# Row-tile order at the seam between the experts and the second block, with the first q projection split by row tiles

## Chip, cores and metric

One core of a Trainium2 chip runs the whole program in one launch. The metric is device time in microseconds. The median of three runs of the kernel before is 2227.41 us.

## What is computed

Three transformer blocks on 256 tokens of width 1024, all in float32. The change lies where the first block ends and the second begins:

```python
# end of the first block (x1: the tokens ahead of the experts, y: their weighted outputs)
x = layer_norm(ALPHA * x1 + g2 * y) * post2_g + post2_b
# start of the second block
xn = rms_norm(x, norm_in_g)
proj = xn @ w_in_2                 # q, k, v, g_ret, x_lru, g_lru: 1024 columns each
q, k = rotary(q), rotary(k) * 128 ** -0.5
xc = causal_depthwise_conv(x_lru, conv_w, conv_b)          # width 4
o_lru = rg_lru(xc, gates)          # the gates are small matmuls on xc
```

## The kernel before, in words

**Tiles.** Rows are tokens. The 256 tokens are two row tiles of 128 partitions (`t` = 0, 1). A weight matrix goes through TensorE in units of 512 columns; `plan()` lists the units in the order in which SyncE loads them (2 MB each, a ring of six slots `W`) and TensorE uses them. Unit number u writes PSUM banks 0 and 1 or 2 and 3 by its parity, and starts once unit u-2 has been read (`unit_free`). `dense(name, lhs)` does one unit; `half_rows_of(name, t, lhs)` does one row tile of a unit, 8 matmuls of 128x512. A float32 matmul stands in the trace as two records, so a unit is 32 records in either form.

**The seam.** The experts leave their sum in PSUM banks 4 to 7 (bank 4+q holds columns 256q to 256q+255 of both row tiles). After the last scatter (L1087):

- VectorE takes the statistics of both tiles (L2162, L2165, L2167), ScalarE the root (`act_std`, L363), VectorE subtracts the mean and applies the gain for both tiles (L2172), then the scale and shift for both (L2178) into `X`.
- `act_rms` (L374, L376) on ScalarE squares and sums each tile of `X` and takes the root; `rms_scale` (L355, L357) on VectorE writes the normed rows to `row(2)`, and each tile raises `rows_ready`.
- TensorE transposes a tile's rows (`row_to_columns`, L797: 8 transposes into banks 4 and 5), and ScalarE copies them out as columns (`copy_columns`, L389: two copies for a tile). The first unit, `xl0`, starts at L654 when the columns of both tiles are there.
- Up to then TensorE fills its time with matmuls whose result nobody reads (`keep_active`, L803).

**Behind the seam** the units run in the order xl0, xl1, gl0, gl1, q20, q21, then eight small gate matmul pairs (L1127) that need the convolution (L2216, L2218 on VectorE, from the copied xl units), then k20 to gr1. VectorE turns q20 by its angles (`rotary`, L2234 to L2242) after the convolution. GpSimd issues the loads of the gate weights when the first block is done (`block1_done`), and of the angle table (`ROT`, L608) when both tiles have raised `rows_ready`.

The engines' programs are written out by hand and run in program order; only semaphores tie them together. `row_in` counts a tile of `X` up for ScalarE, `row_done` a tile of normed rows for TensorE:

```python
for t in range(TT):
    pe.wait_ge(ev("rows_ready"), NORMED["xn"] + t + 1)
    row_to_columns("xn", t, row(2)[:, t])
columns_ready("xn")
for n_ in ("xl0", "xl1", "gl0", "gl1", "q20", "q21"):
    dense(n_, lhs)
```

Of the kernel before, what the change touches and what calls it, by code (L numbers as in the profile page):

```python
# [17 lines left out]
ALU = mybir.AluOpType  # L18
# [3 lines left out]
T = 256  # L22
TT = T // P
D = 1024
KT = D // P
# [5 lines left out]
CONV1, CONV2 = 31, 4  # L31
# [5 lines left out]
LN_EPS, RMS_EPS = 1e-5, 1e-6  # L37
# [60 lines left out]
def plan():  # L98

    units = []  # L100

    def add(name, kind, mat, cols, rows=1):
        units.append((name, kind, [(mat, r * D, c) for c in cols for r in range(rows)]))

    def mod(name, i):
        add(name, "mod", "w_mod", [i * D, i * D + CH])

    mod("sc1", 1)
    mod("sh1", 0)
    for i in range(2):  # L110
        add(f"ag{i}", "col", "w_in", [D + i * CH])
        add(f"av{i}", "col", "w_in", [i * CH])
    for n, base in (("v", 3), ("u", 2), ("ga", 4), ("gb", 5)):
        for i in range(2):
            add(f"{n}{i}", "row", "w_in", [base * D + i * CH])
    for i in range(2):
        add(f"wb{i}", "row", "w_b", [i * CH])
    mod("g1", 2)
    for i in range(2):
        add(f"wa{i}", "row", "w_a", [i * CH])  # L120
    for i in range(2):
        add(f"wo{i}", "row", "w_out", [i * CH])
    mod("sc2", 4)
    mod("sh2", 3)
    mod("g2", 5)
    units.append(("moe", "moe", []))
    for n, base in (("xl", 4), ("gl", 5)):
        for i in range(2):
            add(f"{n}{i}", "col", "w_in_2", [base * D + i * CH])
    for n, base in (("q2", 0), ("k2", 1), ("v2", 2), ("gr", 3)):  # L130
        for i in range(2):
            add(f"{n}{i}", "row", "w_in_2", [base * D + i * CH])
    for i in range(2):
        add(f"w2o{i}", "row", "w_out_2", [i * CH], rows=2)
    add("gq", "col", "gla_w_in_3", [0])
    add("gk", "col", "gla_w_in_3", [CH])
    for i in range(4):
        add(f"gv{i}", "row", "gla_w_in_3", [D + i * CH])
    for i in range(4):
        add(f"gz{i}", "row", "gla_w_in_3", [3 * D + i * CH])  # L140
    for i in range(2):
        add(f"go{i}", "row", "gla_w_out_3", [i * CH], rows=2)
    for i in range(4):
        add(f"su{i}", "col", "s5_w_in_3", [i * CH])
    for i in range(4):
        add(f"sz{i}", "col", "s5_w_in_3", [2 * D + i * CH])
    for i in range(4):
        add(f"sg{i}", "col", "s5_w_glu_3", [i * CH], rows=2)
    for i in range(2):
        add(f"so{i}", "row", "s5_w_out_3", [i * CH], rows=2)  # L150
    return units
# [18 lines left out]
def build(nc, A, out):  # L170
# [11 lines left out]
    TB, n = {}, 0  # L182
# [8 lines left out]
    with ExitStack() as ctx:  # L191
# [33 lines left out]
        def row(i):  # L225
            return flat(i).rearrange("p (t d) -> p t d", t=TT)
# [9 lines left out]
        def pcol(r, n=1):  # L236
            return PC[:, r // P, r % P:r % P + n]
# [12 lines left out]
        def ev(name):  # L250
            if name not in S:
                S[name] = sem(name)
            return S[name]
# [44 lines left out]
        def vector(dve, name):  # L298

            n = vec_at[0]  # L300
            assert VECTORS[n][0] == name, (VECTORS[n], name)
            vec_at[0] += 1
            dve.wait_ge(v_landed[n % NV], 16 * (n // NV + 1))
            return V[:, n % NV, 0:VECTORS[n][2]]
# [34 lines left out]
        def root_taken(dve):  # L339
            norms_out[0] += 1  # L340
            dve.wait_ge(std_ready, norms_out[0])
            dve.reciprocal(RS[:], SD[:])
            dve.drain()

        def row_in(ins):

            rows_in[0] += 1
            ins.then_inc(ev("row_ready"), 1)

        def rms_scale(dve, dst, src, gain, done):  # L350

            for t in range(TT):
                norms_out[0] += 1
                dve.wait_ge(std_ready, norms_out[0])
                dve.reciprocal(RS[:, t:t + 1], SD[:, t:t + 1])  # L355
                dve.drain()
                done(dve.scalar_tensor_tensor(dst[:, t, :], src[:, t, :], RS[:, t:t + 1], gain, ALU.mult, ALU.mult))  # L357
            dve.drain()

        def act_std(act):  # L360
            norms_in[1] += 1
            act.wait_ge(var_ready, norms_in[1])
            act.activation(SD[:], VE[:], ACT.Sqrt).then_inc(std_ready, 1)  # L363

        def act_tile_std(act, t):
            norms_in[1] += 1
            act.wait_ge(var_ready, norms_in[1])
            act.activation(SD[:, t:t + 1], VE[:, t:t + 1], ACT.Sqrt).then_inc(std_ready, 1)
# [9 lines left out]
        def act_rms(act, src, unused):  # L378

            for t in range(TT):  # L380
                act_tile_rms(act, src, unused, t)
# [258 lines left out]
        def _(pe):  # L640
# [150 lines left out]
            def row_to_columns(name, t, src):  # L791
                for h in range(2):
                    n = TB[name] + 2 * t + h
                    if n >= 2:
                        pe.wait_ge(tp_copied, n - 1)
                    for j in range(4):
                        ins = pe.transpose(PS[:, 4 + n % 2, j * P:(j + 1) * P], src[:, (4 * h + j) * P:(4 * h + j + 1) * P], ident)  # L797
                    ins.then_inc(tp_ready, 1)
# [312 lines left out]
            keep_active(0, 6)  # L1111
            pe.wait_ge(ev("row_ready"), 1)
            keep_active(0, 4)
            for t in range(TT):
                pe.wait_ge(ev("rows_ready"), NORMED["xn"] + t + 1)
                row_to_columns("xn", t, row(2)[:, t])
            columns_ready("xn")
            for n_ in ("xl0", "xl1", "gl0", "gl1", "q20", "q21"):
                dense(n_, lhs)
            pe.wait_ge(ev("gate_w_landed"), 64)  # L1120
            pe.wait_ge(ev("xc_ready"), 1)
# [260 lines left out]
        def _(act):  # L1382
# [127 lines left out]
            with act.Fori(0, NE - 1) as e:  # L1510
                expert(e)
            expert(NE - 1)
            act_std(act)

            act_rms(act, X, row(3))
            copy_columns(act, "xn", col(HT))

            def quarter(name):
# [252 lines left out]
        def _(dve):  # L1771
# [6 lines left out]
            def used(ins):  # L1778
                ins.then_inc(v_used, 1)
# [377 lines left out]
            with dve.Fori(0, NE - 1) as e:  # L2157
                expert(e, False)
            expert(NE - 1, True)
            for t in range(TT):  # L2160
                for q in range(4):
                    dve.bn_stats(HST[:, 4 * t + q, :], PS[:, 4 + q, t * T:(t + 1) * T])  # L2162
            dve.drain()
            for t in range(TT):
                dve.bn_aggr(MV[:, t, :], HST[:, 4 * t:4 * t + 4, :].rearrange("p q s -> p (q s)"))  # L2165
            dve.drain()
            dve.tensor_scalar_add(VE[:], MV[:, :, 1], LN_EPS).then_inc(var_ready, 1)  # L2167
            norms_in[0] += 1
            root_taken(dve)
            vec = vector(dve, "post2_g").rearrange("p (q n) -> p q n", q=4)  # L2170
            for t in range(TT):
                ins = dve.scalar_tensor_tensor(X[:, t, :].rearrange("p (q n) -> p q n", q=4), PS[:, 4:8, t * T:(t + 1) * T],  # L2172
                                               MV[:, t, 0:1], vec, ALU.subtract, ALU.mult)
            used(ins)
            dve.drain()
            vec = vector(dve, "post2_b")
            for t in range(TT):
                row_in(dve.scalar_tensor_tensor(X[:, t, :], X[:, t, :], RS[:, t:t + 1], vec, ALU.mult, ALU.add))  # L2178
            dve.drain()
            dve.sem_inc(v_used, 1)  # L2180
            dve.sem_inc(ev("block1_done"), 1)

            def row_done(ins):
                ins.then_inc(ev("rows_ready"), 1)

            dve.wait_ge(ev("gain_landed"), 16)
            rms_scale(dve, row(2), X, TAB2[:], row_done)

            dve.wait_ge(ev("lam_ln"), 1)
            dve.tensor_scalar(LS[:, 2], LS[:, 0], 1.0, -1.0, ALU.add, ALU.add)  # L2190
# [16 lines left out]
            dve.tensor_scalar(LS[:, 4], LS[:, 1], -8.0, None, ALU.mult)  # L2207
            dve.tensor_scalar(LS[:, 5], LS[:, 1], -16.0, None, ALU.mult).then_inc(ev("rates_ready"), 1)

            dve.wait_ge(unit_free[UNIT["xl0"][0] % 2], UNIT["xl0"][0] // 2 + 1)  # L2210
            dve.wait_ge(unit_free[UNIT["xl1"][0] % 2], UNIT["xl1"][0] // 2 + 1)
            for lag in range(CONV2):
                for k in range(KT):
                    w_ = pcol(R_CW2 + (CONV2 - 1 - lag) * KT + k)
                    if lag == 0:
                        ins = dve.tensor_scalar(XC[:, k, :], XLC[:, k, :], w_, pcol(R_CB2 + k), ALU.mult, ALU.add)  # L2216
                    else:
                        ins = dve.scalar_tensor_tensor(XC[:, k, lag:], XLC[:, k, 0:T - lag], w_, XC[:, k, lag:],  # L2218
                                                       ALU.mult, ALU.add)
                if lag == CONV2 - 1:  # L2220
                    ins.then_inc(ev("xc_ready"), 1)
                dve.drain()
            dve.wait_ge(ev("tables_landed"), 80)

            def rotary(name, dst, i):
# [17 lines left out]
                    dve.drain()  # L2243

            rotary("q20", Q2, 0)
            rotary("q21", Q2, 1)
            dve.sem_inc(ev("q_ready"), 1)
            dve.wait_ge(ev("gates_read"), 8)
# [374 lines left out]
```

## Time and profile before

| | |
|---|---|
| runs | 2225.69, 2227.41, 2227.54 us (median 2227.41) |
| profiled execution | 2228.49 us, its span 2226.7 us |
| granted TensorE clock, mean | 0.991 |
| busy: PE, weight loads, DVE, ACT, POOL | 95%, 50%, 35%, 20%, 3% of the span |
| chain that ended last, by engine | PE 75%, ACT 9%, DMA 6%, DVE 5% |
| last scatter ends, first unit of block 2 starts | 1356.2 us, 1370.5 us |

PE is TensorE, DVE VectorE, ACT ScalarE, POOL GpSimd, SP SyncE. Busy time of PE includes the matmuls that nobody reads, so its 95% is not useful work. A granted clock of 1.00 is 2.4 GHz and 0.50 is 1.2 GHz.

### The profile page before, as it was taken

To read this page: it belongs to the slowest core of one execution; us is meant where nothing else is said; L and a number is where in the kernel's file an instruction comes from. 1 tells how busy PE (TensorE), PEld (TensorE's weight loads), DVE (VectorE), ACT (ScalarE), POOL (GpSimd) and SP (SyncE) were. 2 spreads that over 40 slices of the span, in tenths; PEclk is the share of its full clock that TensorE was granted. 3 is DMA by queue.
4 is the path that set the end of the run, shared out by engine and by line. 5 is a ranking of instruction groups with operands and counts; after the bars stand their busy time and mean duration, and the time that the engine had idled before them with its cause. 6 is when DMAs were issued, how large, how long until landed. Compare 5 with 4: busy or idle time off the path is not lost.

```text
span 2226.7 us, 30826 instructions
## 1 busy us (share of the span) xinstructions
PE 2122.8 (95%) x11636; PEld 1102.8 (50%) x11637; DVE 784.1 (35%) x1910; ACT 444.5 (20%) x895; POOL 76.1 (3%) x96
## 2 busy tenths in 40 slices
PE   6999999999999998999999998999999999998998
PEld 5745553333333333333333336745564446887873
DVE  1894362222222222222222223340212354998100
ACT  1011120111011110101101101132012215997100
POOL 0000000000000000000000000000000000222000
PEclk9999998999999999999999999999999999999999
DMA  9754678989999996999989999435234323232340
GB/s 368 262 189 148 247 288 324 418 342 417 372 402 419 418 418 250 417 390 374 417 354 417 418 418 379 159 114 189 76 128 151 113 95 141 78 115 77 138 156 28
DMA packets 157318, 591.33 MB, mean 266 GB/s; under 512 B 5072, under 2 KB 5136, under 8 KB 124352
## 3 DMA queue, kind: packets, MB, share of 16 engines
q1 hardware_dynamic: 152240, 572.03, 65.7%
q0 software_dynamic: 4384, 16.40, 2.0%
q10 hardware_dynamic: 624, 1.93, 0.2%
q8 instruction: 48, 0.79, 0.1%
q14 instruction: 22, 0.18, 0.0%
HBM read 589.29 MB, written 1.05 MB: 265 GB/s over the span
## 4 chain that ended last, share of the span: by engine, by line
PE 75%; ACT 9%; DMA 6%; DVE 5%; DVEq 1%; issue 1%; SPq 1%; ACTq 1%
PE PS L666 19%; PE PS L1054 15%; PE PS L654 9%; PE PS L1075 9%; DMA W<-in_w_gu 5%; PE PS L697 4%; PE PS L681 4%; PE PS L1087 2%; PE PS L1000 2%; ACT BIG L1691 1%; PE PS L1336 1%; PE PS L1045 1%; PE PS L1017 1%; DVE BIG L2076 1%; DVE BIG L2078 1%
## 5 line engine op out<-in xcount | busy, mean ns | idle before, releaser
L1054 PE MATMUL PS<-W,BIG 128*64 128x512 f32 x2048 | 451.0, 597 | 10.7 <-DMA W<-in_w_gu 10.7
L666 PE MATMUL PS<-W,BIG 128*128 128x512 f32 x960 | 417.9, 597 | 4.3 <-DVE BIG L2554 2.9
L666 PEld LDWEIGHTS PS<-W,BIG 128*128 128x128 f32 x960 | 183.2, 191 | 231.3 <-issue 225.8
L1054 PEld LDWEIGHTS PS<-W,BIG 128*64 128x64 f32 x2048 | 143.8, 137 | 300.6 <-issue 279.6
L1075 PE MATMUL PS<-W,BIG 128*64 128x512 f32 x1024 | 226.8, 595 | 2.8
L654 PE MATMUL PS<-BIG,W 128*128 128x256 f32 x896 | 194.5, 380 | 0.7 <-ACT BIG L389 0.7
L654 PEld LDWEIGHTS PS<-BIG,W 128*128 128x128 f32 x896 | 170.2, 190 | 24.5 <-ACT BIG L389 1.0
L1501 ACT ACTIVATE BIG<-BIG 128x512 f32<-128x512 f32 x32 | 20.2, 630 | 717.3 <-DVE BIG L2076 717.3
L2076 DVE TENSOR_SCALAR BIG<-PS 128x512 f32<-128x512 f32 (+1 forms) x38 | 24.7, 650 | 353.5 <-PE PS L1054 331.5
L1075 PEld LDWEIGHTS PS<-W,BIG 128*64 128x64 f32 x1024 | 70.4, 137 | 138.3 <-issue 125.0
L1273 PE MATMUL PS<-BIG,W 128*128 128x256 f32 x512 | 117.0, 382 | 5.0 <-ACT BIG L1658 3.0
L1273 PEld LDWEIGHTS PS<-BIG,W 128*128 128x128 f32 x512 | 94.9, 190 | 20.4 <-issue 7.7
L1841 DVE SCALAR_TENSOR_TENSOR BIG<-BIG,PC 128x255 f32<-128x255 f32 (+29 forms) x240 | 95.4, 464 | 3.8 <-issue 0.5
L697 PE MATMUL PS<-W,BIG 128*128 128x512 f32 x192 | 83.7, 593 | 0.7 <-ACT BIG L389 0.7
L681 PE MATMUL PS<-W,BIG 128*128 128x512 f32 x192 | 83.2, 592 | 0.0
L2118 DVE TENSOR_TENSOR BIG<-PS,BIG 128x512 f32<-128x512 f32 x32 | 22.1, 692 | 163.3 <-PE PS L1075 163.3
L958 PE MATMUL PS<-BIG 128*64 128x512 f32 x264 | 64.4, 609 | 3.9 <-issue 3.5
L1087 PE MATMUL PS<-BIG 64*128 64x256 f32 x512 | 63.9, 389 | 0.0
L1087 PEld LDWEIGHTS PS<-BIG 64*128 64x128 f32 x512 | 46.9, 186 | 30.2 <-issue 26.0
L681 PEld LDWEIGHTS PS<-W,BIG 128*128 128x128 f32 x192 | 36.4, 190 | 44.9 <-issue 44.9
L697 PEld LDWEIGHTS PS<-W,BIG 128*128 128x128 f32 x192 | 36.1, 190 | 43.5 <-issue 42.5
L2301 DVE TENSOR_TENSOR X<-X,PS 128x512 f32<-128x512 f32 x12 | 8.0, 686 | 126.0 <-PE PS L681 65.3
(508 smaller groups left out, 2012.4 us busy)
## 6 DMA issues: line engine op xcount, KB each, us to landing
W<-in_w_gu SPq DMA_DIRECT2D x128, 2048.0 KB, 15.6
W<-in_w_dn SPq DMA_DIRECT2D x64, 2048.0 KB, 16.1
W<-in_w_in SPq DMA_DIRECT2D x24, 2048.0 KB, 17.7
W<-in_w_mod SPq DMA_DIRECT2D x12, 2048.0 KB, 10.9
W<-in_gla_w_in SPq DMA_DIRECT2D x10, 2048.0 KB, 7.9
W<-in_s_w_in SPq DMA_DIRECT2D x8, 2048.0 KB, 8.8
W<-in_s_w_glu SPq DMA_DIRECT2D x8, 2048.0 KB, 8.5
W<-in_w_out SPq DMA_DIRECT2D x6, 2048.0 KB, 7.9
```

What stands on the lines that cost most here:

```text
L654: ins = pe.matmul(ps[:, m // 2, (m % 2) * T:(m % 2 + 1) * T], slot(c0 + i)[:, k, m * P:(m + 1) * P], lhs(i * KT + k), start=i + k == 0, st ...
L666: ins = pe.matmul(ps[:, t, :], lhs(i * KT + k)[:, t * P:(t + 1) * P], w[:, k, :], start=i + k == 0, stop=last_chunk and k == KT - 1)
L681: ins = pe.matmul(ps[:, t, :], lhs(i * KT + k)[:, t * P:(t + 1) * P], w[:, k, :], start=i + k == 0, stop=i == 1 and k == KT - 1)
L697: ins = pe.matmul(unit_ps(name)[:, t, :], lhs(k)[:, t * P:(t + 1) * P], slot(c0)[:, k, :], start=k == 0, stop=k == KT - 1)
L958: ins = pe.matmul(PS[hh[h], 3, :], G[:, t, :], H2[:, t, h * CH:(h + 1) * CH], start=t == 0, stop=t == TT - 1, skip_group_check=True)
L1000: ins = pe.matmul(PS[qq[q], g, 0:T], XETX[:, k, :], gu_w(k)[:, g * D + q * T:g * D + (q + 1) * T], start=False, stop=k == KT - 1, skip_gro ...
L1054: ins = pe.matmul(PS[hh[h], g, :], XET[:, k, :], gu_w(k)[:, g * D + h * CH:g * D + (h + 1) * CH], start=False, stop=k == KT - 1, skip_grou ...
L1075: ins = pe.matmul(PS[hh[h], 2, :], ACTT[:, k, :], dn_w(k)[:, h * CH:(h + 1) * CH], start=k == 0, stop=k == KT - 1, skip_group_check=True)
L1087: ins = pe.matmul(PS[:, 4 + q, t * T:(t + 1) * T], SC[r, t * P:(t + 1) * P], YE[r, (q % 2) * T:(q % 2 + 1) * T], start=False, stop=False, ...
L1273: ins = pe.matmul(PS[:, bank, part * T:(part + 1) * T], slot(c0)[:, k, m * P:(m + 1) * P], lhs(k), start=k == 0, stop=k == KT - 1, skip_gr ...
L1841: ins = dve.scalar_tensor_tensor(cv[:, k, lag:], ya[:, k, 0:T - lag], pcol(r), cv[:, k, lag:], ALU.mult, ALU.add)
L2076: dve.tensor_scalar(GT[:, w], PS[:, 0, w], 7.0, None, ALU.min).then_inc(clipped, 1)
```

## The change

- `plan()`: q20 becomes the first unit of the second block, ahead of xl0. All later units of that group but q21 move back by one place, in load order and in PSUM parity.
- VectorE does the layer norm and the RMS norm row tile by row tile: `moments(t)`, `centred(t)`, `scaled(t)`, `normed(t)` in the order m0, c0, s0, m1, c1, n0, s1, n1. ScalarE's roots follow, one for each tile.
- TensorE: transposes of tile 0, the first half of q20 (tile 0), transposes of tile 1, the second half of q20, then xl0, xl1, gl0, gl1, q21.
- VectorE: the rotation of q20 stands ahead of the convolution.

```diff
@@ plan @@
     units.append(("moe", "moe", []))
+    add("q20", "row", "w_in_2", [0])
     for n, base in (("xl", 4), ("gl", 5)):
...
     for n, base in (("q2", 0), ("k2", 1), ("v2", 2), ("gr", 3)):
-        for i in range(2):
+        for i in range(n == "q2", 2):
@@ TensorE @@
             keep_active(0, 4)
-            for t in range(TT):
-                pe.wait_ge(ev("rows_ready"), NORMED["xn"] + t + 1)
-                row_to_columns("xn", t, row(2)[:, t])
+            pe.wait_ge(ev("rows_ready"), NORMED["xn"] + 1)
+            row_to_columns("xn", 0, row(2)[:, 0])
+            pe.wait_ge(tp_copied, TB["xn"] + 2)
+            half_rows_of("q20", 0, lhs)
+            pe.wait_ge(ev("rows_ready"), NORMED["xn"] + 2)
+            row_to_columns("xn", 1, row(2)[:, 1])
             columns_ready("xn")
-            for n_ in ("xl0", "xl1", "gl0", "gl1", "q20", "q21"):
+            half_rows_of("q20", 1, lhs)
+            for n_ in ("xl0", "xl1", "gl0", "gl1", "q21"):
                 dense(n_, lhs)
@@ ScalarE @@
-            act_std(act)
-            act_rms(act, X, row(3))
+            act_tile_std(act, 0)
+            act_tile_rms(act, X, row(3), 0)
+            act_tile_std(act, 1)
+            act_tile_rms(act, X, row(3), 1)
             copy_columns(act, "xn", col(HT))
@@ VectorE @@
+            def moments(t):
+
                 for q in range(4):
                     dve.bn_stats(HST[:, 4 * t + q, :], PS[:, 4 + q, t * T:(t + 1) * T])
...
+            def centred(t):
+
+                dve.scalar_tensor_tensor(X[:, t, :].rearrange("p (q n) -> p q n", q=4), PS[:, 4:8, t * T:(t + 1) * T],
+                                         MV[:, t, 0:1], gain.rearrange("p (q n) -> p q n", q=4), ALU.subtract, ALU.mult)
...
+            moments(0)
+            centred(0)
+            scaled(0)
+            moments(1)
+            centred(1)
+            dve.wait_ge(ev("gain_landed"), 16)
...
+            normed(0)
+            scaled(1)
+            dve.drain()
+            dve.sem_inc(v_used, 2)
+            dve.sem_inc(ev("block1_done"), 1)
+            normed(1)
...
             rotary("q20", Q2, 0)
+            dve.wait_ge(unit_free[UNIT["xl0"][0] % 2], UNIT["xl0"][0] // 2 + 1)
+            dve.wait_ge(unit_free[UNIT["xl1"][0] % 2], UNIT["xl1"][0] // 2 + 1)
+            for lag in range(CONV2):
...
             rotary("q21", Q2, 1)
```

How the instructions stand now. First TensorE (PE) at the start of the second block, before: L803 is `keep_active`, L797 the transposes, L654 the matmuls of xl0. A row counts matmuls, not trace records.

```order
L803 MATMUL PS<-K 128x256 x3
L797 MATMUL PS<-K,BIG 128x128 [waits tp_copied,rows_ready]
L797 MATMUL PS<-K,BIG 128x128 x3
L797 MATMUL PS<-K,BIG 128x128 [waits tp_copied]
L797 MATMUL PS<-K,BIG 128x128 x3
L797 MATMUL PS<-K,BIG 128x128 [waits tp_copied,rows_ready]
L797 MATMUL PS<-K,BIG 128x128 x3
L797 MATMUL PS<-K,BIG 128x128 [waits tp_copied]
L797 MATMUL PS<-K,BIG 128x128 x3
L654 MATMUL PS<-BIG,W 128x256 [waits w_landed0,unit_free0,tp_copied]
```

The same place in the changed kernel, where the lines are one further down and L698 is half a unit of q20:

```order
L804 MATMUL PS<-K 128x256 x3
L798 MATMUL PS<-K,BIG 128x128 [waits tp_copied,rows_ready]
L798 MATMUL PS<-K,BIG 128x128 x3
L798 MATMUL PS<-K,BIG 128x128 [waits tp_copied]
L798 MATMUL PS<-K,BIG 128x128 x3
L698 MATMUL PS<-W,BIG 128x512 [waits w_landed0,unit_free0,tp_copied]
L698 MATMUL PS<-W,BIG 128x512 x7
L798 MATMUL PS<-K,BIG 128x128 [waits tp_copied,rows_ready]
L798 MATMUL PS<-K,BIG 128x128 x3
L798 MATMUL PS<-K,BIG 128x128 [waits tp_copied]
L798 MATMUL PS<-K,BIG 128x128 x3
L698 MATMUL PS<-W,BIG 128x512 [waits tp_copied]
```

The transposes of tile 1 have moved behind the first half of q20, and the second half waits for their copies.

ScalarE (ACT) at the same place in the changed kernel: L369 is the root of the layer norm, L375 and L377 the square sum and the root of the RMS norm, L390 the four copies of columns, L1529 the copies of xl0 and xl1.

```order
L369 ACTIVATE SD<-VE 128x1 [waits var_ready]
L375 ACTIVATE BIG,VE<-X 128x1024 [waits row_ready]
L377 ACTIVATE SD<-VE 128x1
L369 ACTIVATE SD<-VE 128x1 [waits var_ready]
L375 ACTIVATE BIG,VE<-X 128x1024 [waits row_ready]
L377 ACTIVATE SD<-VE 128x1
L390 ACTIVATE BIG<-PS 128x4x128 [waits tp_ready] x4
L1529 ACTIVATE BIG<-PS 128x1024 [waits chunk_done] x2
```

The four copies stand behind both tiles' square sums, as they did before.

VectorE (DVE) from the last scatter on in the changed kernel: L2169 to L2173 are the moments, L2180 `centred`, L2187 and L2189 `scaled`, L2205 and L2207 `normed`.

```order
L2169 BN_STATS HST<-PS 128x6 x3
L2171 BN_AGGR MV<-HST 128x2
L2173 TENSOR_SCALAR VE<-MV 128x1
L2180 SCALAR_TENSOR_TENSOR X<-PS,MV,V 128x1024
L2187 RECIPROCAL RS<-SD 128x1 [waits std_ready]
L2189 SCALAR_TENSOR_TENSOR X<-X,RS,V 128x1024
L2169 BN_STATS HST<-PS 128x6 x4
L2171 BN_AGGR MV<-HST 128x2
L2173 TENSOR_SCALAR VE<-MV 128x1
L2180 SCALAR_TENSOR_TENSOR X<-PS,MV,V 128x1024
L2205 RECIPROCAL RS<-SD 128x1 [waits std_ready,gain_landed]
L2207 SCALAR_TENSOR_TENSOR BIG<-X,RS,TAB2 128x1024
```

Tile 0's normed rows now come ahead of the scaling of tile 1, which with tile 1's own normed rows follows behind this piece.

## Rows read from the trace of the kernel before

**Rows 1.** The page: span, and the chain that ended last, by engine.

```profile
span 2226.7 us, 30826 instructions
...
PE 75%; ACT 9%; DMA 6%; DVE 5%; DVEq 1%; issue 1%; SPq 1%; ACTq 1%
```

**Rows 2.** Timeline from 1352 us: start us, us, engine line op names shapes count [idle before].

```profile
1356.25 2.75 DVE L2162 BATCH_NORM_STATS2 HST<-PS 128x6 f32<-128x256 f32 x8 [2.62 <-PE PS L1087]
1359.08 0.39 DVE L2165 BATCH_NORM_AGGREGATE MV<-HST 128x2 f32<-128x24 f32 x2
1359.55 0.17 DVE L2167 TENSOR_SCALAR VE<-MV 128x2 f32<-128x2 f32 x1
...
1360.23 2.48 DVE L2172 SCALAR_TENSOR_TENSOR X<-PS,MV,V 128x1024 f32<-128x1024 f32 x2
1362.80 2.48 DVE L2178 SCALAR_TENSOR_TENSOR X<-X,RS,V 128x1024 f32<-128x1024 f32 x2
1364.12 1.06 ACT L374 ACTIVATE BIG<-X 128x1024 f32<-128x1024 f32 x1 [4.17 <-DVE X L2178]
1364.14 2.00 PE L803 MATMUL PS<-K 128*128 128x256 f32 x8 [1.28 <-DVE X L2178]
...
1365.34 0.20 ACT L376 ACTIVATE SD<-VE 128x1 f32<-128x1 f32 x1
...
1365.64 0.16 DVE L355 RECIPROCAL RS<-SD 128x1 f32<-128x1 f32 x1 [0.36 <-ACT SD L376]
...
1365.88 1.28 DVE L357 SCALAR_TENSOR_TENSOR BIG<-X,RS,TAB 128x1024 f32<-128x1024 f32 x1
...
1367.22 1.09 PE L797 MATMUL PS<-K,BIG 128*128 128x128 f32 x8 [1.08 <-DVE BIG L357]
1367.91 1.08 ACT L389 ACTIVATE BIG<-PS 128x512 f32<-128x512 f32 x2 [1.06 <-PE PS L797]
1368.93 0.70 POOL L608 DMA_DIRECT2D TAB<-in_k_rot  x1
1369.34 1.08 ACT L389 ACTIVATE BIG<-PS 128x512 f32<-128x512 f32 x2 [0.35 <-PE PS L797]
```

**Rows 3.** The chain of waits, 1350 to 1480 us: start us, us, what.

```profile
1370.48 55.52 PE PS L654 x256
1426.00 27.47 PE PS L666 x64
```

**Rows 4.** DMA issues, 1360 to 1400 us: names, queue, count, KB, us to landing.

```profile
TAB<-in_k_rot POOLq DMA_DIRECT2D x1, 128.0 KB, 8.9
```

**Rows 5.** Timeline of VectorE behind the seam.

```profile
1402.30 9.88 DVE L2218 SCALAR_TENSOR_TENSOR BIG<-BIG,PC 128x255 f32<-128x255 f32 x24
1439.85 0.42 DVE L2234 TENSOR_TENSOR BIG<-PS,TAB 128x256 f32<-128x256 f32 x1 [27.67 <-PE PS L666]
```

**Rows 6.** Timeline of TensorE, 1795 to 1812 us.

```profile
1800.18 1.04 PE L1225 MATMUL PS<-K,BIG 128*128 128x128 f32 x8
1802.79 1.09 PE L1225 MATMUL PS<-K,BIG 128*128 128x128 f32 x8 [1.57 <-DVE BIG L2387]
1804.62 7.97 PE L666 MATMUL PS<-W,BIG 128*128 128x512 f32 x14 [0.74 <-ACT BIG L1606]
```

**Rows 7.** Stretches of 1 us: length, busy by engine, then PEclk, DMA share, GB/s.

```profile
1805.00:1806.00 1.00, 1.00 (x2) 0.34 (x1) 0.00 (x0) 0.99 (x2) 1.00 (x3) 0.51 0.00 0
...
1808.00:1809.00 1.00, 1.00 (x4) 0.37 (x3) 1.00 (x1) 0.00 (x0) 1.00 (x3) 0.79 0.93 369
```

**Rows 8.** The chain of waits, 1800 to 1836 us.

```profile
1804.62 29.43 PE PS L666 x64
```

**Rows 9.** An earlier pause of TensorE: timeline, and two stretches of 1 us.

```profile
362.67 3.68 PE L958 MATMUL PS<-BIG 128*64 128x512 f32 x8 [3.55 <-issue]
...
361.00:362.00 1.00, 0.00 (x0) 0.00 (x0) 0.00 (x0) 0.00 (x0) 0.00 (x0) 0.59 0.97 410
...
367.00:368.00 1.00, 1.00 (x6) 0.80 (x4) 0.00 (x0) 0.56 (x1) 0.00 (x0) 0.50 0.28 49
```

More of the change, by code:

```diff
@@ L2159, in _ @@
             expert(NE - 1, True)
-            for t in range(TT):
+            def moments(t):
                 for q in range(4):
                     dve.bn_stats(HST[:, 4 * t + q, :], PS[:, 4 + q, t * T:(t + 1) * T])
-            dve.drain()
-            for t in range(TT):
+                dve.drain()
                 dve.bn_aggr(MV[:, t, :], HST[:, 4 * t:4 * t + 4, :].rearrange("p q s -> p (q s)"))
-            dve.drain()
-            dve.tensor_scalar_add(VE[:], MV[:, :, 1], LN_EPS).then_inc(var_ready, 1)
@@ L2168, in _ @@
[L2168 to L2178, printed above, removed]
@@ L2179, in _ @@
-            dve.drain()
-            dve.sem_inc(v_used, 1)
-            dve.sem_inc(ev("block1_done"), 1)
+                dve.drain()
+                dve.tensor_scalar_add(VE[:, t:t + 1], MV[:, t, 1:2], LN_EPS).then_inc(var_ready, 1)
+                norms_in[0] += 1
+            gain, shift = vector(dve, "post2_g"), vector(dve, "post2_b")
+            def centred(t):
+                dve.scalar_tensor_tensor(X[:, t, :].rearrange("p (q n) -> p q n", q=4), PS[:, 4:8, t * T:(t + 1) * T],
+                                         MV[:, t, 0:1], gain.rearrange("p (q n) -> p q n", q=4), ALU.subtract, ALU.mult)
@@ L2183, in row_done, with scaled @@
+            def scaled(t):
+                norms_out[0] += 1
+                dve.wait_ge(std_ready, norms_out[0])
+                dve.reciprocal(RS[:, t:t + 1], SD[:, t:t + 1])
+                dve.drain()
+                row_in(dve.scalar_tensor_tensor(X[:, t, :], X[:, t, :], RS[:, t:t + 1], shift, ALU.mult, ALU.add))
+            moments(0)
[4 more added lines that the diff above has]
+            dve.wait_ge(ev("gain_landed"), 16)
             def row_done(ins):
@@ L2184, in row_done, with normed @@
                 ins.then_inc(ev("rows_ready"), 1)
-            dve.wait_ge(ev("gain_landed"), 16)
-            rms_scale(dve, row(2), X, TAB2[:], row_done)
+            def normed(t):
+                norms_out[0] += 1
+                dve.wait_ge(std_ready, norms_out[0])
+                dve.reciprocal(RS[:, t:t + 1], SD[:, t:t + 1])
+                dve.drain()
+                row_done(dve.scalar_tensor_tensor(row(2)[:, t, :], X[:, t, :], RS[:, t:t + 1], TAB2[:], ALU.mult, ALU.mult))
+                dve.drain()
@@ L2189, in _ @@
+            normed(0)
+            scaled(1)
+            dve.drain()
+            dve.sem_inc(v_used, 2)
+            dve.sem_inc(ev("block1_done"), 1)
+            normed(1)
             dve.wait_ge(ev("lam_ln"), 1)
@@ L2208, in _ @@
             dve.tensor_scalar(LS[:, 5], LS[:, 1], -16.0, None, ALU.mult).then_inc(ev("rates_ready"), 1)
[L2210 to L2222, printed above, removed]
             dve.wait_ge(ev("tables_landed"), 80)
@@ L2245, in _ @@
             rotary("q20", Q2, 0)
+            dve.wait_ge(unit_free[UNIT["xl0"][0] % 2], UNIT["xl0"][0] // 2 + 1)
+            dve.wait_ge(unit_free[UNIT["xl1"][0] % 2], UNIT["xl1"][0] // 2 + 1)
+            for lag in range(CONV2):
+                for k in range(KT):
+                    w_ = pcol(R_CW2 + (CONV2 - 1 - lag) * KT + k)
+                    if lag == 0:
+                        ins = dve.tensor_scalar(XC[:, k, :], XLC[:, k, :], w_, pcol(R_CB2 + k), ALU.mult, ALU.add)
+                    else:
+                        ins = dve.scalar_tensor_tensor(XC[:, k, lag:], XLC[:, k, 0:T - lag], w_, XC[:, k, lag:],
+                                                       ALU.mult, ALU.add)
+                if lag == CONV2 - 1:
+                    ins.then_inc(ev("xc_ready"), 1)
+                dve.drain()
             rotary("q21", Q2, 1)
```

## Prediction

> **What bounds the kernel now.** I read the page first: of a span of 2226.7 us the chain that ended last is 75% TensorE's, with short pieces of ScalarE and VectorE between [rows 1]. So the question is where TensorE waits and whether the edit shortens that wait. Then the timeline at the seam: the last scatter releases VectorE at 1356.25, and useful matmuls begin again at 1370.48 [rows 2, 3]. Between them lies one serial thread, 14.2 us long: statistics, two passes over X, square sum, normed rows, transposes, copies. The matmuls of L803 in it are filler. From 1370.48 on the chain is matmuls without a gap (55.52 us, then 27.47 us) [rows 3], so whatever the seam costs or saves arrives whole at the end. All other stages keep their code; their loads and waits hang on finished units and shift with them.
>
> **VectorE, tile by tile.** Eight statistics take 2.75 us, so four take about 1.4; the aggregate is about 0.26 (half of 0.39 and a start-up), the sum with epsilon 0.17, each with some 0.08 us of drain ahead [rows 2]. Moments of tile 0 end at 1356.25 + 2.0 = 1358.3. The root now runs beside `centred(0)`, which is 1.2 us (half of 2.48), to 1359.5. A reciprocal takes 0.24 to the start of its pass (1365.64 to 1365.88) and the pass 1.28: X of tile 0 is done at 1360.9. Moments of tile 1 add 1.9 (1362.8), `centred(1)` 1.2 (1364.0), `normed(0)` 1.5: tile 0's rows stand at 1365.5, against 1367.2 before. `scaled(1)` ends at 1367.0.
>
> **ScalarE, where the head start is lost.** TensorE transposes tile 0 from 1365.5, with both banks ready by 1366.6 (1.09 us [rows 2]). But in ScalarE's program the copies stand behind the square sum and root of tile 1, which wait for `scaled(1)`. From L374's start to L376's end is 1365.54 - 1364.12 = 1.42 us [rows 2], so that root ends at 1367.0 + 1.4 = 1368.5. Two copies take 1.08, and TensorE resumes 0.06 later (1370.42 to 1370.48 [rows 2, 3]): the first half of q20 starts at 1369.6, 0.9 us earlier than work started before. Tile 1's rows come at 1368.5 + 0.1 + 0.24 + 1.28 = 1370.1, later than before but well ahead of need.
>
> **TensorE, what the split adds.** Half a unit is a quarter of the 27.47 us for two units [rows 3], 6.87 us: to 1376.5. Now come the transposes of tile 1, with nothing else to do meanwhile. From a tile's first transpose to the end of its copies is 1367.22 to 1368.99, 1.77 us [rows 2], plus 0.06: the second half starts at 1378.3. Taking off the 6.87 us of work already done, this is as if the block had started at 1371.4, where it started at 1370.48 before. **The order of events alone costs 1.0 us**: -0.9 from the start, +1.8 from a turn of tile 1 that can no longer overlap VectorE, rounded.
>
> **The clock.** Filler ends at about 1364.0: its groups of 7, 6 and 4 matmuls are 34 records, and at 2.00 us for 8 [rows 2] they last some 8 us from 1356.1, now end to end, since both signals between them (root 1358.5, X of tile 0 1360.9) come before they are waited for. Then TensorE idles 1.5 us, transposes 1.1 us, idles 3.0 us (1366.6 to 1369.6), and starts dense work. Before, its waits in the seam were 1.28 us at most [rows 2], with filler or transposes between them, and dense work ran at its full pace from the first record (27.47 us for two units [rows 3]). The nearest row is at 1800: transposes, idle 1.57, transposes 1.09, idle 0.74, then dense matmuls [rows 6], and the clock went to 0.51 in the stretch from 1805 and came back within the one from 1808 [rows 7], 3.4 us in all. The 64 matmul records behind that pause took 29.43 us [rows 8] and the same number at full clock 27.47 [rows 3]: 1.96 us lost. The new pause is emptier than that one, so I take the clock to fall here too, and **2.0 us** as the price. The bounds: 0, if it holds; and from the pause of 3.55 us at 359, after which the clock was low from the stretch 361 (0.59) through the one of 367 (0.50) [rows 9], some 6.8 us, which all under dense work would cost 3.4. In its section "Terms", the Trainium skill's page "TensorE: Matmul & The Clock Gate" puts the penalty at the throttled time times (1 - K/N), half of it at half clock. By that rule the low stretch at 1805 should have cost 1.7 us where the row shows 1.96, and the sum would be 0.3 us smaller; the measured row is the one used.
>
> **What lies beside other work.** The rotation of q20 costs nothing on the path. It was 4.6 us on VectorE between 1439.85 and q21's; now it must be done before xl1 may take q20's PSUM banks, at about 1378.3 + 6.9 + 13.9 = 1399. It can start at 1385.2 if the angle table has landed: POOL issued that at 1368.93 and it took 8.9 us [rows 2, 4]; 1.4 us later it lands near 1379, 6 us early. If it came 9 us late, xl1 would begin to wait. The convolution (12.6 us, of which 9.88 in L2218) starts when xl1 is copied, near 1415, and the gates need it near 1456; VectorE idled 27.67 us behind it [rows 5]. The gate weights are issued 1.4 us later and have over 80 us. Weights: q20 takes the slot that xl0 had, loaded long before. Filler matmuls still write bank 0 ahead of the first unit, as before.
>
> **Sum.** +1.0 + 2.0 = +3.0 us. The profiled execution's 2228.49 becomes 2231.5; it stands 1.1 us above the median of the runs, and on that median of 2227.41 the forecast is **2230.4 us**. A measurement of this kernel can tell some 0.2% from no change, 4.45 us, so this counts as no change, with a sign that I expect to be plus.
>
> **Rivals.**
> - *The clock holds* (0.15). For it: before, with both tiles' transposes in the same place, it held. Against: the pause now holds one tile's and is longer. Then only +1.0: 2228.4.
> - *The clock falls twice* (0.15, the slower side). The split makes a second pause, 1.1 us of transposes and 0.7 idle, right behind a stretch that is itself at low clock; either the low stretch is a long one as at 361 (3.4 us), or it falls again behind the second pause (2.0 more). 1.0 + 3.4 = 4.4 gives 2231.8, with both 6.4 gives 2233.8. It counts as slower from 3.45 us of clock loss, 6.9 us of low clock under dense work. For it: the pause at 359 led to a long one [rows 9]. Against: the pause at 1804 had one low stretch of 3.4 us and dense work raised the clock.
> - *The head start arrives* (0.04). If the copies of tile 0 got ahead of the square sum of tile 1, the first half would start near 1367.3 and the second lose 1.8: 1.4 us faster, 2226.0. Both engines' programs say otherwise: ScalarE's copies stand behind it. Even this is within 0.2%; nothing in the seam is worth 4.5 us, as tile 0's rows come only 1.7 us earlier.
> - *The change does not split* (0.02): TensorE might wait for both tiles before the first half. The order of instructions rules it out.
> - *A late table* or another wait that I have not seen (0.04): from 9 us of lateness on xl1 stalls, 1 us for 1 us.
>
> The forecast itself, one fall at 1.4 to 3.4 us, has 0.60.
>
> **Numbers.** The range runs from the clock that holds, with 1 us of scatter between runs as shown before (2225.69 to 2227.54), 2227.4, to two falls without the long one, 2233.0. Faster by over 0.2% 0.03; slower by over 0.2%, from the second rival's upper part and unseen waits, 0.14; the rest 0.83.
>
> **What would show it.** In the profile of the changed kernel: tile 0's normed rows 1.7 us earlier after the last scatter; a first copy on ScalarE whose idle time is not ended by a transpose, but which follows L377 directly; 3 us without matmuls ahead of L698; a granted clock of 0.5 soon after; 1.8 us between the two halves of q20; from xl0 to the end the old durations. The forecast is wrong if the clock stays at 1.00 through the first half, if the copies come before tile 1's root, or if any wait for q20's rotation appears ahead of xl1.

## The result and the profile after

The change takes 2231.03 us (median of 12 runs, 2228.02 to 2235.70), the kernel before beside it 2226.80 us (12 runs, 2223.03 to 2227.56). The ratio is 1.0021, with a 95% interval of 1.0013 to 1.0030: slower by 4.7 us, between 2.9 and 6.7. Measured again with the experiments (11 runs against 33) it was 1.0011, 1.0002 to 1.0020. The forecast was 2230.4 us, +3.0 us, and +3.0 us lies inside both intervals. Both intervals stand clear of no change. The prediction gave 0.14 to a loss of over 0.2%; the first ratio is at that line, and its interval reaches to both sides of it.

The profiled execution of the change took 2228.71 us, only 0.2 us more than that of before. That does not contradict the medians; the last part of this section shows why. First the seam. The chain of waits of the changed kernel, 1345 to 1480 us (start us, us, what):

```profile
1353.48 0.02 issue
1353.50 0.43 DVE HST L2169
...
1361.38 1.28 DVE BIG L2207
...
1362.99 1.30 DVE X L2189
1364.29 0.02 issue
1364.31 1.06 ACT BIG L375
...
1365.53 0.20 ACT SD L377
1365.73 0.98 ACT BIG L390 x2
1366.71 0.04 issue
1366.76 9.44 PE PS L698 x16
1376.19 0.45 PE PS L798 x4
...
1376.67 1.09 ACT BIG L390 x2
1377.76 0.04 issue
1377.81 7.13 PE PS L698 x16
1384.94 55.25 PE PS L655 x256
```

The chain goes from `scaled(1)` (L2189) through ScalarE's square sum and root of tile 1 (L375, L377) to the copies of tile 0's columns (L390) and only then to q20's first half (L698). Before, the corresponding chain ran from L374 to L389 and L654 [rows 2, 3]. The timeline shows the pause that this leaves on TensorE, and that nothing but program order keeps the copies back (the second column is the duration, brackets hold the idle time before):

```profile
1353.38 7.61 PE L804 MATMUL PS<-K 128*128 128x256 f32 x34
...
1362.72 1.09 PE L798 MATMUL PS<-K,BIG 128*128 128x128 f32 x8 [1.73 <-DVE BIG L2207]
...
1365.53 0.20 ACT L377 ACTIVATE SD<-VE 128x1 f32<-128x1 f32 x1
...
1365.64 1.07 ACT L390 ACTIVATE BIG<-PS 128x512 f32<-128x512 f32 x2
...
1366.76 9.44 PE L698 MATMUL PS<-W,BIG 128*128 128x512 f32 x16 [2.95 <-ACT BIG L390]
```

TensorE has transposed tile 0 by 1363.8, and the first copy starts at 1365.64 with no idle time in front of it: it follows the root L377 at once. TensorE waits 2.95 us. Its clock, in stretches of 1 us (length, busy by engine, PEclk, DMA share, GB/s):

```profile
1364.00:1365.00 1.00, 0.00 (x0) 0.00 (x0) 0.28 (x1) 0.69 (x1) 0.28 (x1) 0.80 1.07 393
...
1370.00:1371.00 1.00, 1.00 (x2) 0.34 (x1) 0.00 (x0) 0.00 (x0) 0.29 (x1) 0.50 1.01 307
1371.00:1372.00 1.00, 1.00 (x3) 0.51 (x2) 0.00 (x0) 0.00 (x0) 0.00 (x0) 0.79 1.05 324
```

The granted clock fell to 0.50 (1.2 GHz) at 1364.6, in the pause, and came back at 1371.4. The first half of q20 took 9.44 us where the second half, which also starts behind a pause but at full clock, took 7.13 us in the chain above: 2.3 us lost. (Half a unit in an unbroken stream takes 6.87 us, 27.47 / 4 [rows 3]. At full clock a group that starts behind a pause takes 0.26 us more than that, so 6.87 is not the figure to compare with.)

From here on I use one figure for every kernel, the **seam**: from the first statistic after the last scatter to the start of the first unit that is dense in both tiles behind q20, less the 13.73 us which q20 takes. For before it is 1370.48 - 1356.25 = 14.2 us; for the change 1384.78 - 1353.50 - 13.73 = 17.5 us. So the seam is 3.3 us longer.

**Why the two profiled executions are equal nevertheless.** The change's last scatter already came 2.75 us earlier than before's (first statistic at 1353.50 against 1356.25 [rows 2]), in code that was not touched. The reason is the clock again. One place of several: early in the program, where the experts begin, it was low for 10.2 us in the profile of before and for 3.4 us in that of the change. First the ends of that stretch before:

```profile
337.00:338.00 1.00, 1.00 (x4) 0.81 (x4) 0.78 (x6) 0.00 (x0) 0.00 (x0) 0.64 1.07 426
347.00:348.00 1.00, 1.00 (x6) 0.38 (x4) 0.00 (x0) 0.00 (x0) 0.00 (x0) 0.74 0.00 0
```

Then the change's, which began in the stretch from 340 (PEclk 0.80) and was over at 344.0:

```profile
340.00:341.00 1.00, 1.00 (x5) 0.27 (x6) 0.75 (x5) 0.00 (x0) 0.00 (x0) 0.80 1.01 406
```

Apart from one at the very start and one at the very end, a profile has four to seven such stretches, and how many there are and how long each lasts differs from one execution to the next. Up to the seam the time follows them: over all thirteen profiles kept, whose code up to there is the same, the first statistic behind the last scatter comes between 1352.2 us (13.0 us of low clock under matmuls before it) and 1359.7 us (26.4 us), about 0.5 us for each us of low clock. The spread of whole runs goes with the clock too: of 33 runs of the kernel before, the 13 whose mean granted clock was 0.993 took 2227.2 us on average, the 7 at 0.991 took 2229.9. The mean over its 33 runs is 0.9923, over the change's 12 runs 0.9903.

### The profile page after: what moved, and what is told of

Same layout as the page of the kernel before. It is cut to its first block, busy times and chain, and to the rows that moved or that the text cites. A ratio compares the mean times of both kernels' runs of the same rounds, so it can differ in the third digit from the quotient of the medians.

```text
span 2226.9 us, 30833 instructions
## 1 busy us (share of the span) xinstructions
PE 2120.9 (95%) x11636; PEld 1101.8 (49%) x11637; DVE 785.3 (35%) x1912; ACT 444.9 (20%) x896; POOL 76.1 (3%) x96
## 4 chain that ended last, share of the span: by engine, by line
PE 75%; ACT 9%; DMA 6%; DVE 5%; DVEq 2%; issue 1%; SPq 1%; ACTq 1%
PE PS L667 18%; PE PS L1055 15%; PE PS L655 9%; PE PS L1076 9%; DMA W<-in_w_gu 5%; PE PS L698 4%; PE PS L682 4%; PE PS L1088 2%; PE PS L1001 2%; ACT BIG L1697 1%; PE PS L1341 1%; PE PS L1046 1%; PE PS L1018 1%; DVE BIG L2082 1%; DVE BIG L2084 1%
## 5 line engine op out<-in xcount | busy, mean ns | idle before, releaser
L1055 PE MATMUL PS<-W,BIG 128*64 128x512 f32 x2048 | 450.4, 596 | 10.9 <-DMA W<-in_w_gu 10.9
L698 PE MATMUL PS<-W,BIG 128*128 128x512 f32 x224 | 100.2, 605 | 4.4 <-ACT BIG L390 4.4
L698 PEld LDWEIGHTS PS<-W,BIG 128*128 128x128 f32 x224 | 42.8, 194 | 55.8 <-issue 50.7
```

Of the source, the lines that this page charges most:

```text
L698: ins = pe.matmul(unit_ps(name)[:, t, :], lhs(k)[:, t * P:(t + 1) * P], slot(c0)[:, k, :], start=k == 0, stop=k == KT - 1)
L1055: ins = pe.matmul(PS[hh[h], g, :], XET[:, k, :], gu_w(k)[:, g * D + h * CH:g * D + (h + 1) * CH], start=False, stop=k == KT - 1, skip_grou ...
```

## Experiments

Theory A is the prediction's: the loss is the order of events in the seam, and the low clock behind TensorE's pause. Theory B puts it behind the seam, into the new order of units and of the rotation. Theory C blames the split of q20. Each experiment had 11 or 12 runs. Kernels that were measured together share the 29 to 33 runs of the kernel before that stood beside them. "Low under work" is the time at 0.5 of the clock in which matmuls of the seam ran, in the one profiled execution of each. The expectations take the seam to the second half of q20, less 6.9 us; that gives 0.1 us less for the change.

| kernel | ratio to before (95% interval) | seam, us | low under work, us |
|---|---|---|---|
| change | 1.0021 (1.0013 to 1.0030) | 17.5 | 4.7 |
| change, again | 1.0011 (1.0002 to 1.0020) | 18.0 | 5.7 |
| copies of tile 0 first | 0.9991 (0.9982 to 1.0000) | 14.7 | 3.4 |
| change with filler | 1.0009 (1.0000 to 1.0018) | 15.2 | 0 |
| norms only | 1.0016 (1.0007 to 1.0025) | 19.6 | 8.0 |
| split only | 1.0000 (0.9991 to 1.0009) | 14.8 | 0 |
| copies first, filler | 0.9989 (0.9980 to 0.9998) | 13.0 | 0 |
| + turn inside the half | 0.9994 (0.9985 to 1.0003) | 12.0 | 0 |
| + early rows | 0.9990 (0.9981 to 0.9999) | 10.9 | 0 |
| + early rows, again | 0.9983 (0.9974 to 0.9992) | 10.9 | 0 |
| + filler elsewhere | 0.9976 (0.9967 to 0.9985) | 10.9 | 0 |
| before, filler elsewhere | 0.9991 (0.9982 to 0.9999) | 14.2 | 0 |

**The change again.** The same kernel, no edit.

> The changed kernel itself, on the same chip as the three that follow. Theory A: its runs lie about 3 to 4 us above the kernel before, their mean granted clock is lower by 0.001 to 0.002 than that of the runs of before, and the seam in its profile is 14.9 us plus half of the time at low clock that falls under work. If instead its mean clock is the same as before's, the low clock in one profile was chance and the loss has another cause.

Its runs lie 2.4 us above before (0.4 to 4.5), less than the 3 to 4 us expected, though the interval covers them. Their mean clock is 0.9909 against 0.9923, as expected; a stretch of 6.8 us at half clock makes 0.0015 of a span of 2227 us. The seam is 18.0 us, where 14.9 + 5.7 / 2 = 17.8 was expected. Its first half of q20:

```profile
1365.44 9.96 PE L698 MATMUL PS<-W,BIG 128*128 128x512 f32 x16 [2.95 <-ACT BIG L390]
```

The fall of the clock in the seam is in both profiles of the change, and the lower mean clock of the runs fits it.

**Copies of tile 0 first.** ScalarE alone (`copy_tile`, not shown, does the two of `copy_columns`' four copies that belong to one tile):

```diff
             act_tile_std(act, 1)
+            copy_tile(act, "xn", col(HT), 0)
             act_tile_rms(act, X, row(3), 1)
-            copy_columns(act, "xn", col(HT))
+            copy_tile(act, "xn", col(HT), 1)
```

> The changed kernel with ScalarE's two copies of tile 0's columns moved ahead of the square sum of tile 1. Call seam the time from the first statistic after the last scatter to the start of q20's second half, less the 6.9 us of its first half (for the kernel before: to the start of xl0, 14.2 us; for the change 17.4 us in its profile). Theory A (the loss is the order of events in the seam plus the low clock behind TensorE's 3 us pause): the first half starts 11.0 us after the first statistic, where the change had 13.3, the pause is 0.7 us, the seam 12.9 us if the clock holds and up to 2 us more if it falls, so 1.3 us faster to 0.7 us slower than the kernel before. Theory B (the loss lies behind the seam, in the new order of units and of the rotation): the seam gets shorter by 2 us or more, but the time stays 2 us or more above the kernel before.

Two lines of order remove the loss: the ratio is 0.9991. That this kernel is faster than before is not shown by its seam, which is still 0.5 us longer. The timeline of this kernel:

```profile
1361.48 1.09 PE L807 MATMUL PS<-K,BIG 128*128 128x128 f32 x8 [1.72 <-DVE BIG L2217]
...
1362.17 1.08 ACT L389 ACTIVATE BIG<-PS 128x512 f32<-128x512 f32 x2 [3.13 <-PE PS L807]
...
1363.31 8.83 PE L707 MATMUL PS<-W,BIG 128*128 128x512 f32 x16 [0.74 <-ACT BIG L389]
```

Now the copies wait for the transposes and TensorE for 0.74 us only; the first half starts 11.0 us after the first statistic (1352.27), as worked out. But behind idle times of 1.72 and 0.74 us the clock still fell in this profile and was low from 1363.6 to 1367.1. Theory B is out: the units and the rotation stand as in the change, and the loss is gone.

**The change with filler.** TensorE alone:

```diff
-            keep_active(0, 4)
+            keep_active(0, 7)
             pe.wait_ge(ev("rows_ready"), NORMED["xn"] + 1)
             row_to_columns("xn", 0, row(2)[:, 0])
+            keep_active(0, 6)
             pe.wait_ge(tp_copied, TB["xn"] + 2)
```

> The changed kernel with filler matmuls in TensorE's two pauses (three more ahead of the transposes of tile 0, six between them and the first half of q20) and nothing else. Theory A: the order of events is unchanged, so the first half still starts 13.3 us after the first statistic, but the clock holds, the first half takes 6.9 us instead of 9.4, the seam is 15.1 us: 0.9 us slower than the kernel before, and the runs scatter less than the change's did (7.7 us from lowest to highest). Theory B: no difference from the change beyond noise, 4 us slower than before.

The timeline of this kernel:

```profile
1366.59 1.09 PE L798 MATMUL PS<-K,BIG 128*128 128x128 f32 x8 [0.42 <-DVE BIG L2208]
...
1367.52 2.75 PE L804 MATMUL PS<-K 128*128 128x256 f32 x12
...
1370.63 7.13 PE L698 MATMUL PS<-W,BIG 128*128 128x512 f32 x16 [0.35 <-ACT BIG L390]
```

In the same place the clock, in stretches of 2 us:

```profile
1366.00:1368.00 2.00, 1.57 (x12) 1.36 (x12) 1.83 (x3) 0.00 (x0) 0.00 (x0) 1.00 1.05 388
1368.00:1370.00 2.00, 2.00 (x11) 1.67 (x9) 0.44 (x3) 1.75 (x5) 1.41 (x2) 1.00 1.04 384
1370.00:1372.00 2.00, 1.65 (x5) 0.68 (x4) 1.75 (x6) 0.58 (x2) 2.00 (x4) 1.00 1.06 389
```

The first half starts 13.25 us after the first statistic, exactly as in the change (13.26), so the order of events is the same; the filler removes only the fall of the clock, and the seam drops from 17.5 to 15.2 us. That separates the two terms: 15.2 - 14.2 = 1.0 us is the order, the rest the clock. The runs agree in size (+2.0 us, 0 to 4.0) but cannot prove it alone, as their interval touches that of the change. They span 5.7 us where the change's spanned 7.7, as expected, but that says little: the 33 runs of before span 8.8, with the clock low in other places.

**Norms only.** Norms tile by tile and q20 in front, but whole:

```diff
-            half_rows_of("q20", 0, lhs)
...
-            half_rows_of("q20", 1, lhs)
-            for n_ in ("xl0", "xl1", "gl0", "gl1", "q21"):
+            for n_ in ("q20", "xl0", "xl1", "gl0", "gl1", "q21"):
```

> Norms tile by tile and q20 in front, but the split of q20 undone: both tiles are transposed first, then whole units run. Theory A: tile 1's normed rows come 13.8 us after the first statistic (12.4 before), so the first unit starts at 15.7, 1.4 us later than before; TensorE has 3 us without matmuls between the two sets of transposes, so the clock may fall for up to 2.6 us more: 1.4 to 4 us slower than before. Theory C (the split, not the norms, costs the time): within 1 us of the kernel before.

The timeline of this kernel:

```profile
1366.13 1.09 PE L798 MATMUL PS<-K,BIG 128*128 128x128 f32 x8 [1.73 <-DVE BIG L2203]
...
1370.75 1.97 PE L798 MATMUL PS<-K,BIG 128*128 128x128 f32 x8 [3.53 <-DVE BIG L2203]
...
1373.41 16.96 PE L667 MATMUL PS<-W,BIG 128*128 128x512 f32 x32 [0.69 <-ACT BIG L390]
```

Of all kernels the longest pause (3.53 us) and the longest seam: the clock was low for 10.2 us, twice the transposes' usual time and 16.96 us for a unit of 13.73. Half of the 8.0 us under work is 4.0, which leaves 15.6 us for the order, 1.4 more than before, as expected. The clock was expected to cost at most 2.6 us, so the seam came out 1.3 us above the bound. Its 11 runs lie close together (2230.16 to 2233.43, ten of them at a mean clock of 0.990). Theory C is out: without the split the loss is no smaller.

**Split only.** The norms of before, for both tiles together, with q20 split and in front, and its rotation ahead of the convolution. The edit is the change's own in `plan()`, on TensorE and for the rotation, without its parts for the norms:

> The split of q20, its place in front and the rotation ahead of the convolution, but the norms for both tiles together as before. Theory A: copies of tile 0 end 12.8 us after the first statistic, the turn of tile 1 behind the first half adds 1.8, the seam is 14.6 us, the longest pause is under 1.3 us and the clock holds: 0.4 us slower than before. Theory C (the split costs the time) and theory B (the new order behind the seam does): 3 us or more slower than before.

The timeline of this kernel:

```profile
1364.81 1.09 PE L798 MATMUL PS<-K,BIG 128*128 128x128 f32 x8 [1.09 <-DVE BIG L358]
...
1366.64 7.13 PE L698 MATMUL PS<-W,BIG 128*128 128x512 f32 x16 [0.74 <-ACT BIG L390]
```

Seam 14.8 us (14.6 expected), no fall in this profile, and a ratio of 1.0000. The first half starts 12.8 us after the first statistic, earlier than in the change, because tile 1's square sum is done when the copies are due. The head start of tile-by-tile norms was thus negative as wired.

**Towards a faster kernel.** Three more, each on top of the previous: filler added to "copies first" (7 instead of 4 ahead of the transposes, 1 behind); the transposes of tile 1 after four of the eight matmuls of the first half; and `normed(0)` ahead of `centred(1)` with tile 0 transposed into banks 2 and 3, five matmuls ahead of tile 1's transposes. The last one also goes back to 4 pieces of filler ahead of the transposes, so it is not purely an addition. The core of the second and third edits together, with the third's numbers:

```diff
-            half_rows_of("q20", 0, lhs)
+            part_rows_of("q20", 0, lhs, range(0, 5))
             pe.wait_ge(ev("rows_ready"), NORMED["xn"] + 2)
             row_to_columns("xn", 1, row(2)[:, 1])
+            part_rows_of("q20", 0, lhs, range(5, KT))
             columns_ready("xn")
...
             moments(1)
-            centred(1)
             dve.wait_ge(ev("gain_landed"), 16)
...
             normed(0)
+            centred(1)
             scaled(1)
```

> Copies of tile 0 ahead of tile 1's square sum, as in the first experiment, and filler in both pauses (three more matmuls ahead of the transposes, one between them and the first half). Theory A: seam 12.9 us with the clock held, where the first experiment had 14.7 with its clock low in the seam; 1.3 us faster than before. If the filler does nothing, the same as the first experiment.

> The previous kernel with the transposes of tile 1 in the middle of the first half of q20 (after four of its eight matmuls), so that their copies run beside the other four. Theory A: only the 1.1 us of the transposes is left of the 1.8 us turn, seam 12.1 us, 2.1 us faster than before. If the copies are not what TensorE waits for between the halves, no gain over the previous kernel.

> In addition tile 0's normed rows ahead of the mean subtraction of tile 1, with its transposes in banks 2 and 3 (banks 4 and 5 still hold tile 1's sums), and five matmuls of the first half ahead of tile 1's transposes. Theory A: tile 0's rows 8.1 us after the first statistic instead of 9.2, the seam 11.1 us, 3.1 us faster than before. If tile 1's rows become the bound, 12 us or more.

The seams came out at 13.0, 12.0 and 10.9 us where 12.9, 12.1 and 11.1 were expected. The filler took 1.7 us off the seam of "copies first" (14.7 to 13.0), half of the 3.4 us for which the clock was low in that profile. The last one's timeline:

```profile
1367.73 1.09 PE L817 MATMUL PS<-K,BIG 128*128 128x128 f32 x8 [0.57 <-DVE BIG L2228]
...
1369.56 4.56 PE L707 MATMUL PS<-W,BIG 128*128 128x512 f32 x10 [0.30 <-ACT BIG L389]
...
1373.95 1.04 PE L817 MATMUL PS<-K,BIG 128*128 128x128 f32 x8
...
1374.83 2.74 PE L707 MATMUL PS<-W,BIG 128*128 128x512 f32 x6
```

Between the transposes of tile 1 and the rest of the half there is no wait left. The whole runs (0.9989, 0.9994, 0.9990) confirm that all three are at or below before, but not the steps of 1 us between them: the interval is about 2 us to either side. So that order rests on the seams alone.

**Filler elsewhere.** In the eleven profiles without it, dense work behind the transposes at about 1801 us met a low clock in seven, and so0 at about 2161 in eight. Filler there:

```diff
+            keep_active(6, 3)
             turn_head(3)
+            keep_active(6, 1)
             columns_ready("og")
...
+            keep_active(6, 5)
             pe.wait_ge(ev("glu_ready"), 4)
```

> The kernel with the shortest seam so far (early rows, turn of tile 1 inside the first half), and filler matmuls in two pauses of TensorE far from the seam where the traces showed the clock fall: around the last transposes of the gated values near 1801 us (three and one) and ahead of so0 near 2160 us (five). Theory A (a pause costs the clock wherever dense work follows it): the clock holds at both places, up to 2 us less at each, so 4 to 7 us faster than before and a mean clock about 0.002 higher. If filler only helps by luck of the run: 2 to 3 us faster, as without it.

> The kernel before with only those two fillers. Theory A: 2 to 4 us faster than before by the clock alone, the seam unchanged at 14.2 us. Otherwise no difference.

> The kernel with the shortest seam once more, beside the two above. Theory A: 3.1 us faster than before by its seam of 11 us; its first five rounds gave 0.1% with an interval of 0.1% on either side.

In both kernels that have it the clock held at both places in the one profile of each. But both profiles have a low stretch (6.8 and 3.4 us) near 1636 us, in code ahead of this filler, where none of the other eleven has one; no run shows why. The timeline of "+ filler elsewhere" at the first place (compare [rows 6]):

```profile
1801.95 1.46 PE L823 MATMUL PS<-K 128*128 128x256 f32 x6
1803.68 1.09 PE L1251 MATMUL PS<-K,BIG 128*128 128x128 f32 x8 [0.27 <-DVE BIG L2440]
1804.61 0.60 PE L823 MATMUL PS<-K 128*128 128x256 f32 x2
```

And its clock, in stretches of 4 us, at both places:

```profile
1800.00:1804.00 4.00, 3.73 (x20) 2.48 (x19) 1.29 (x2) 2.00 (x3) 0.00 (x0) 1.00 0.00 0
...
2158.00:2162.00 4.00, 4.00 (x19) 3.19 (x17) 0.52 (x1) 2.10 (x5) 0.00 (x0) 1.00 0.23 35
```

On the kernel before it gives 0.9991 (-2.0 us, interval -4.0 to -0.2), with a mean clock of 0.9932 against 0.9922. With the short seam it gives 0.9976, 5.3 us faster than before (3.3 to 7.3), at a mean clock of 0.9932, 0.001 higher where 0.002 was expected. The short seam by itself gave 0.9983 and 0.9990. The interval of 0.9983, measured beside it, reaches over 0.9976, so what this filler adds to the short seam is not shown by the runs.

## Why the prediction was right

- **Tile 0's rows 1.7 us earlier.** Measured from the first statistic: 10.9 us before (1367.16 [rows 2]), 9.2 in the change (1362.66). Right.
- **The head start lost on ScalarE, 0.9 us left.** The first half was forecast 13.35 us after the first statistic; it came at 13.26, against 14.23 for xl0 before. "Copies first" shows the cause, not only the place: moving the copies alone brings the first half forward by 2.2 us.
- **The turn of tile 1 between the halves, 1.8 us.** From the first transpose (1376.03) to the second half (1377.81) it is 1.78 us.
- **The sum of the order, +1.0.** 15.2 against 14.2 us with the clock held: 1.0.
- **The clock, 2.0 us, bounds 0 and 3.4.** The term that was mis-sized, inside its bounds. The low stretch was of the long kind (6.8 us) in both profiles, with 4.7 and 5.7 us of it under work, and the first half took 9.44 and 9.96 us instead of 7.13: 2.3 and 2.8 us lost. The seams say the same: 17.5 and 18.0 against 15.2 us with the clock held. I had taken the price from the pause at 1800, whose stretch lasted 3.4 us, though the pause was longer here and nearer to that of [rows 9]. With 2.3 to 2.8 the sum is +3.3 to +3.8 and the forecast 2230.7 to 2231.2.

  The price itself was also misread from its row. The 29.43 us at 1804.62 start behind a pause, the 27.47 us that I compared them with do not. In the six profiles in which the clock held at that place the same 64 records take 27.73 us. The chain of "copies first":

```profile
1801.20 27.73 PE PS L676 x64
```

  So the low stretch there cost 29.43 - 27.73 = 1.7 us, not 1.96. Two errors of opposite sign met in the 2.0: the wrong comparison added 0.26 us, the short stretch took 0.6 to 1.1 off. That the first made the second smaller is luck: with the row read rightly the forecast would have been +2.7 us. By the Trainium skill's rule ("TensorE: Matmul & The Clock Gate", section "Terms"), half of the low time under work, the stretch at 1805 costs 1.7 us and the two in the seam 2.3 and 2.9; the traces (1.7, 2.3 and 2.8) agree with it. The prediction's remark that the row shows more than the rule came from the wrong comparison.
- **Rotation and loads hidden.** VectorE starts the rotation at 1385.05, and xl1 finds its banks free: the units behind the second half run 55.25 us without a gap. Before it was 55.52 [rows 3], the 0.27 us more being those of a group that starts behind a pause. That it stands ahead of the convolution costs nothing, and is not optional: xl1 needs the banks of q20, and the convolution needs xl1.
- **The rivals.** That the clock holds did not occur in either profile of the change. "Falls twice" was half right: the long stretch came and cost 2.3 and 2.8 us instead of the 3.4 allowed, a second fall behind the turn of tile 1 did not come. "The head start arrives" needed the other order on ScalarE, and with it and a held clock gave 1.2 us in the seam, where 1.4 was worked out.

What stays open: which of the two measurements (1.0021 and 1.0011) is nearer to the truth. The seam says +3.3 and +3.8 us for single executions. Also open is how often the clock falls in the seam: it did in both profiles of the change, and for the other executions there is only their mean clock. And no run shows which pause is enough for a fall; the kernels show falls and holds, not the condition between them.

## What to carry over

When work is split by tile on one engine, walk through the program order of every other engine that takes part: here the first tile was ready 1.7 us earlier and a copy of 1.1 us stood behind the second tile's turn, so almost half of it was lost and TensorE sat in a pause whose price at the clock (2.3 to 2.8 us) was larger than the prize. To price a low clock, compare a group behind a pause with the same group behind a pause at full clock. A split also turns an overlapped step (the second tile's transposes and copies) into a serial one, unless work of the first tile is kept back to cover it. Where single executions differ by more than the effect, measure the stage from a fixed event to a fixed event, and compare terms there.

## What the runs showed of the hardware

- Idle times of 1.72 and 0.74 us, with 1.1 us of transposes between them, were followed by a fall of the granted clock in one profile ("copies first"). In "split only" 1.28 us at most ahead of each piece of filler or transposes, and 0.74 behind them, were not. Each is a single profile.
- The low stretches between a program's start and its end lasted 3.4, 6.8 or 10.2 us; the place near 338 us took each of these lengths in different profiles, and none in two. What they cost was half of the time that fell under matmuls, so two executions of one program differ by several us (1352.2 to 1359.7 us at the same point of the code).
- Filler matmuls that nobody reads cost no time of their own where TensorE waits anyway (the first half of q20 starts 13.25 us after the first statistic with them, 13.26 without), and kept the clock at 1.00 wherever they were tried: in the seam in six profiles, at the two other places in two.
